# Neighbourhood attention: row sums divided out by GpSimd ahead of the transposes instead of behind the product with V

## The reference, cut to what matters

```python
def hybrid_layer(x, g, w_in, w_out, ...):
    h = rms_norm(x, g)
    z = jnp.einsum('bsd,de->bse', h, w_in)
    ...
    o_da = diff_attention(qd, kd, vd, lam, lam_init, subln_g)
    o_na = neighbourhood_attention(qn, kn, vn, rpb)
    o = jnp.concatenate([o_da, o_na], axis=-1) * jax.nn.silu(gate)
    return x + jnp.einsum('bse,ed->bsd', o, w_out)

    # neighbourhood_attention, for each row of the grid:
    s = q @ kb * scale + bias, masked to the window
    p = jax.nn.softmax(s, axis=-1)
    o = jnp.einsum('bhnqrk,brnkhd->bnqhd', p.astype(v.dtype), vb)
```

## Time and profile before

| what | value |
|---|---|
| median of the runs shown | 1445.77 us (1444.89 to 1445.82) |
| profiled execution, its own time | 1445.27 us |
| span of the profile | 1443.5 us |
| TensorE matmul busy | 1423.7 us, 99% of the span |
| VectorE / ScalarE / GpSimd busy | 882.7 / 687.5 / 494.1 us |
| granted TensorE clock, mean | 0.996 |
| chain that ended last | TensorE 92%, VectorE 3%, ScalarE 2% |

### The profile page before, as it was taken

The page is one execution under the profiler, slowest core; times in us unless marked ns, Lnnn a source line. Parts: engine busy times, 40 slices in busy tenths (PEclk is TensorE's granted clock), DMA queues, the critical chain, the costliest instruction groups (busy, mean ns, idle before and its releaser), DMA issues.

```text
span 1443.5 us, 23727 instructions
## 1 busy us (share of the span) xinstructions
PE 1423.7 (99%) x8180; PEld 1161.4 (80%) x8180; DVE 882.7 (61%) x1827; ACT 687.5 (48%) x1309; POOL 494.1 (34%) x384
## 2 busy tenths in 40 slices
PE   9999999999999999999999999999999999999996
PEld 7788888887888888787887888888878888887875
DVE  6767677667556565653337677666776565656433
ACT  6545554555444444552515554545454444447231
POOL 3223223233333333443642231323233333237152
PEclk9999999999999999999999999999999999999998
DMA  4700101121111111311110110100202121213113
GB/s 182 153 30 27 46 22 36 36 62 38 55 45 49 49 46 47 132 30 58 58 44 30 38 37 15 44 29 22 77 23 63 38 62 36 63 38 124 44 59 117
DMA packets 40698, 79.57 MB, mean 55 GB/s; under 512 B 18992, under 2 KB 19248, under 8 KB 40624
## 3 DMA queue, kind: packets, MB, share of 16 engines
q1 hardware_dynamic: 40480, 78.60, 17.5%
q10 hardware_dynamic: 144, 0.01, 0.0%
HBM read 66.57 MB, written 15.96 MB: 57 GB/s over the span
## 4 chain that ended last, share of the span: by engine, by line
PE 92%; DVE 3%; ACT 2%; DMA 1%; issue 1%; POOL 1%; SPq 0%; POOLq 0%; DVEq 0%; ACTq 0%
PE proj L1041 18%; PE proj L1043 18%; PE proj L1042 18%; PE scores L1077 11%; PE turn L1134 7%; PE mix L1186 3%; PE mix L1187 3%; PE mix L1150 2%; PE mix L1152 2%; PE mix L1151 2%; PE scores L1134 2%; PE mix L1160 1%; DVE pt_lo L1551 1%; DMA xt<-x_t 1%; ACT pt_hi L851 1%
## 5 line engine op out<-in xcount | busy, mean ns | idle before, releaser
L1041 PE MATMUL proj<-h_hi,w_hi 128*128 128x512 f32 x1184 | 491.5, 415 | 2.1 <-DVE h_lo L1426 1.0
L1043 PE MATMUL proj<-h_hi,w_lo 128*128 128x512 f32 x1184 | 465.4, 393 | 0.0
L1042 PE MATMUL proj<-h_lo,w_hi 128*128 128x512 f32 x1184 | 461.8, 390 | 0.0
L626 POOL TENSOR_TENSOR w_lo<-w_raw,w_hi 128x1024 fp32r<-128x1024 f32 x62 | 152.8, 2465 | 502.1 <-ACT w_hi L809 502.1
L1551 DVE TENSOR_TENSOR pt_lo<-turn,pt_hi 128x512 fp32r<-128x512 f32 x208 | 139.1, 669 | 232.2 <-ACT pt_hi L851 231.5
L1043 PEld LDWEIGHTS proj<-h_hi,w_lo 128*128 128x128 f32 x1184 | 222.1, 188 | 50.7
L1041 PEld LDWEIGHTS proj<-h_hi,w_hi 128*128 128x128 f32 x1184 | 223.0, 188 | 47.5 <-issue 9.4
L1042 PEld LDWEIGHTS proj<-h_lo,w_hi 128*128 128x128 f32 x1184 | 223.8, 189 | 34.8
L851 ACT ACTIVATE pt_hi<-turn 128x512 fp32r<-128x512 f32 x208 | 120.2, 578 | 231.0 <-PE turn L1134 229.3
L1543 DVE CUSTOM_DVE_ANT_0 prob<-scores,inner 128x1024 f32<-128x1024 f32 (+1 forms) x192 | 203.5, 1060 | 3.1 <-PE scores L1077 2.7
L876 ACT ACTIVATE prob<-prob,nm,escale_now 128x1024 f32<-128x1024 f32 x128 | 158.4, 1237 | 60.3 <-DVE nm L1547 59.8
(11 more groups left out here) (185 smaller groups left out, 2265.0 us busy)
## 6 DMA issues: line engine op xcount, KB each, us to landing
w_raw<-chunks SPq DMA_DIRECT2D x80, 512.0 KB, 3.5
mixed_dram<-gate SPq DMA_DIRECT2D x28, 256.0 KB, 2.2
edge<-bias_dram SPq DMA_DIRECT2D x32, 224.0 KB, 4.9
h_lo<-mixed_dram SPq DMA_DIRECT2D x14, 512.0 KB, 6.7
xt<-x_t SPq DMA_DIRECT2D x8, 512.0 KB, 8.4
out_t<-xt SPq DMA_DIRECT2D x16, 256.0 KB, 2.1
bias_dram<-bias_rows SPq DMA_DIRECT2D x16, 240.0 KB, 6.1
dist_dram<-inner SPq DMA_DIRECT2D x1, 480.0 KB, 6.5
```

What stands on the lines that cost most here:

```text
L626: pool.tensor_tensor(w_lo[:, b], w_raw[:], f32(w_hi[:, b]), ALU.subtract).then_inc(w_lo_done, 1)
L1041: pe.matmul(dst, a_hi, b_hi, start=start, stop=False)
L1042: pe.matmul(dst, a_hi, b_lo, start=False, stop=False)
L1043: return pe.matmul(dst, a_lo, b_hi, start=False, stop=stop)
```

## The change

GpSimd multiplies the probabilities of each NA tile, both heads, by the reciprocals of their row sums in place (`weigh_rows`), and `turn_p` waits for that product instead of for the exponential. The spread copies, the transposes of the reciprocals and VectorE's product with the gate are dropped. `weigh_rows` stands at the head of GpSimd's step.

```diff
@@ -105,8 +105,6 @@
         for t in range(1, NT + 1):
             for c in range(3 if na and INNER[t - 1] else 2):
                 use(("T", t - 1, c), True)
-            if na and t % 2 == 0:
-                use(("R", t // 2 - 1), False)
         return order, split
 
     def half(t):
@@ -422,7 +420,7 @@
         factor_in = sem("factor_in")
         tails_zero = sem("tails_zero")
         pair_done = sem("pair_done")
-        wide_done = sem("wide_done")
+        prob_scaled = sem("prob_scaled")
 
         f32 = lambda t: t.bitcast(F32)
         HR = NT + NT + 1
@@ -664,18 +662,14 @@
                 pool.wait_ge(gate_plus, 2 * g.group() + t + 1)
                 pool.tensor_tensor(gate[:, cols], gate[:, cols], gate_tanh[:], ALU.mult).then_inc(gate_silu, 1)
 
-            def widen(g, t, before=None):
+            def weigh_rows(g, t):
 
 
                 pool.wait_ge(rrec_done, g.step(t) + 1)
-                if t == 0 and not before.na:
-                    pool.wait_ge(factor_mm, before.kind_pairs(PAIRS - 1) + 1)
-                elif t % 2 == 0:
-                    last = g.use("R", t // 2 - 1) if t else before.use("R", PAIRS - 1)
-                    pool.wait_ge(turned, last + 1)
                 begin(pool, "pool")
-                pool.tensor_copy(rrec_wide[:, t % 2].rearrange("p (m e) -> p m e", e=HD),
-                                 rrec[:, t % 4, :].unsqueeze(2).to_broadcast([P, 2, HD])).then_inc(wide_done, 1)
+                for m in range(2):
+                    part = prob_of(True, t, m, 0, WIDTH[t])
+                    pool.tensor_scalar(part, part, rrec[:, t % 4, m:m + 1], None, ALU.mult).then_inc(prob_scaled, 1)
 
             def normalise(g, p):
 
@@ -688,6 +682,8 @@
 
             def attend(g, behind):
                 for t, front, ft in steps(g, behind):
+                    if front and front.na:
+                        weigh_rows(front, ft)
                     if front and front.projects(ft) and ft % 2 == 0:
                         w_lo_part(front.chunk(ft) + 1, 1 - front.buffer(ft))
                     if g.project and t <= 2:
@@ -696,8 +692,6 @@
                         row_lo(g.l, i)
                     if not behind and t in LAST_CHUNKS:
                         out_lo_part(g.l, LAST_CHUNKS[t])
-                    if front and front.na and t < NT:
-                        widen(front, ft)
                     if t == 1 and not g.project:
                         silu(g, 0)
                     if t == 3 and not g.project:
@@ -710,8 +704,6 @@
                         mask_edge(g.l, behind.i)
                     if t == NT and not g.na:
                         normalise(g, PAIRS - 1)
-                    if front and front.na and t == NT:
-                        widen(front, ft, g)
 
             def norm_stats(n):
                 pool.wait_ge(stat_done, n + 1)
@@ -1121,7 +1113,7 @@
             def turn_p(g, t, c):
                 dst = turn_wait(g, "T", t, c)
                 if g.na:
-                    reached(pe, exp_done, 2 * g.step(t) + min(c, 1) + 1)
+                    pe.wait_ge(prob_scaled, 2 * g.tiles(t) + min(c, 1) + 1)
                 else:
                     pe.wait_ge(comb_done, g.kind_step(t) + 1)
                 if c == 2:
@@ -1187,16 +1179,6 @@
                         last = pe.matmul(out, weights, pt_lo[:, m, at], start=False, stop=n == len(parts) - 1)
                 return last
 
-            def turn_r(g, t):
-
-
-
-                dst = turn_wait(g, "R", t // 2)
-                pe.wait_ge(wide_done, g.tiles(t) + 1)
-                for a in range(2):
-                    last = pe.transpose(dst[:, a * P:(a + 1) * P], rrec_wide[:, a], ident[:])
-                last.then_inc(turned, 1)
-
             def out_piece(l, t, ks):
 
                 n, end = out_number(l, t), NT - 1 if t < EARLY else NT
@@ -1257,8 +1239,6 @@
                     turn_p(g, t - 1, 2)
                 fill(2)
                 if t % 2 == 0:
-                    if g.na:
-                        turn_r(g, t - 1)
                     weigh(g, t - 1)
                 if last_step:
                     turn_v(behind, 0)
@@ -1390,7 +1370,7 @@
                         three(proj[:, q % 2], w_hi[:, b, t // 2], w_lo[:, b, t // 2], h_hi[:, NT - 1, half(t)],
                               h_lo[:, NT - 1, half(t)]).then_inc(piece_done, 1)
                 last_group = Group(l, True, NA_G - 1, project=False)
-                reached(pe, turn_freed, last_group.use("R", PAIRS - 1) + 1)
+                reached(pe, turn_freed, last_group.use("T", NT - 1, 2) + 1)
                 pe.wait_ge(pair_done, last_group.pairs(PAIRS - 1) + 1)
                 if l + 1 == DEPTH:
                     odd = HALVES_LAST[-3:]
@@ -1583,13 +1563,6 @@
                     dve.scalar_tensor_tensor(prob[:, b, :], prob[:, 2, :], cmix[:, b:b + 1], prob[:, b, :],
                                              ALU.mult, ALU.add).then_inc(comb_done, 1)
 
-            def scaled(g, t):
-
-                src, cols = turn_bank(True, ("R", t // 2))[:, 0:2 * P], pair_cols(True, t)
-                dve.wait_ge(turned, g.use("R", t // 2) + 1)
-                dve.wait_ge(gate_silu, 2 * g.group() + TILE[True][t] // 4 + 1)
-                dve.tensor_tensor(gate[:, cols], src, gate[:, cols], ALU.mult).then_inc(turn_freed, 1)
-
             def output_pair(g, t):
 
                 n, cols = (g.l * NA_G + g.i) * PAIRS + t // 2, pair_cols(True, t)
@@ -1597,7 +1570,7 @@
                 dve.tensor_tensor(u_pair[0:HD], mix[0:HD, 0:2 * P], u_pair[0:HD], ALU.add)
                 dve.tensor_tensor(u_pair[HD:P], mix[HD:P, 2 * P:4 * P], u_pair[HD:P], ALU.add).then_inc(u_done, 1)
                 dve.wait_ge(u_done, n + 1)
-                reached(dve, turn_freed, g.use("R", t // 2) + 1)
+                dve.wait_ge(gate_silu, 2 * g.group() + TILE[True][t] // 4 + 1)
                 dve.tensor_tensor(gate[:, cols], u_pair, gate[:, cols], ALU.mult).then_inc(pair_done, 1)
 
             def gated(g, p):
@@ -1659,7 +1632,6 @@
                     piece_part(front, ft)
                 add_pieces(2)
                 if g.na and t % 2 == 0:
-                    scaled(g, t - 1)
                     output_pair(g, t - 1)
                 add_pieces(3)
                 if g.na and t == 1:
```

## The result

The changed kernel takes 1471.66 us (median of four runs, 1469.27 to 1474.47) against 1445.80 us: 25.9 us slower, ratio 1.018, interval 1.0168 to 1.0193. The forecast was 1461.0 us, at most 1470. The direction was right and the size was not.

The account below looks back on a forecast made before the run. TensorE was taken as the bound in ordinary groups, with GpSimd nearly without slack in last groups. Last groups +21.2 us, less 6.0 us taken off TensorE, gave +15.2 us: 1461.0 us, range 1451 to 1470.

Parts of the forecast that it names:

- What bounds the kernel, and where the change binds: TensorE bounds ordinary groups; in each layer's last group GpSimd's rows reach TensorE with 0.4 to 2.4 us to spare.
- What comes off: Transposes of the reciprocals leave TensorE: 26 pairs of 0.23 us not hidden by waits, -6.0 us.
- Ordinary groups hide the products and all that is queued behind them: In ordinary groups, products have 2.3 us to spare and GpSimd work starting up to 3 us later costs nothing.
- The product: One in-place product on GpSimd takes 1.50 us for 512 columns and 1.65 us for 576.
- The nearest row: Profile row for adding a constant over 512 columns on GpSimd, 1497 ns, taken as the product's time.
- the bound from the two copies: Lower estimate of GpSimd's product from copies of 128 and 256 columns: 0.6 us for 512 columns.
- The walk: Tile-by-tile timeline of each last group, products ahead of rows: TensorE shifts 10.6 us a layer, +21.2 us in all.
- The clock: In the last groups TensorE stays busy over two thirds of the time, so no clock fall entered the sum.
- The rival: Clock falls behind last-group waits, 1.9 us each, one or two a layer: 1465 to 1469 us; 0.20 with slower product.
- Most of it isn't the 12 us of products but their place: The last groups' shift comes mostly from rows waiting on GpSimd behind the reciprocals, not from the products' length.

Follow-up runs that it names:

- Run 1: The changed kernel without products in the last group of each layer, whose probabilities stay undivided: 1441.26 us against 1445.49 for the kernel before.
- run 7: The changed kernel with all products on VectorE instead of GpSimd, in ordinary groups too: 1447.91 us, ratio 1.0015.
- run 2: The changed kernel with idle transposes on TensorE ahead of rows 0, 2 and 4 in the last groups, to keep the clock up: 1464.83 us.
- run 4: The changed kernel with every product cut to 64 columns and 34 idle transposes ahead of row 2 in each last group: 1452.27 us.
- run 3: The changed kernel with every product cut to 64 columns, order and waits unchanged: 1456.58 us, ratio 1.0079.

## Why the prediction was wrong, step by step

- **What bounds the kernel, and where the change binds:** right. TensorE is at full clock and without slack in ordinary groups; in both last groups GpSimd has next to no slack. Run 1 places the whole loss there.
- **What comes off, 6.0 us:** right in its working, 3.03 us of 2.99 between the two last groups and 5.52 of 5.52 up to the second, the latter with luck. By the end 4.2 us (medians) or 4.9 us (spans) are left. The prediction had nothing that could take a gain back behind the last group, such as the wait of 0.5 us in run 1.
- **Ordinary groups hide the products and all that is queued behind them:** right. No wait for them there, and run 7 makes no difference by taking the products off GpSimd.
- **The product, 1.50 and 1.65 us:** measured 1.575 and 1.728 us, both some 5% above. The nearest row was the right one, and the bound from the two copies, 0.6 us for 512 columns, was of no use: 64 columns alone take 0.44 us.
- **The walk, 10.6 us a layer:** the mechanism and the waits were right, the term was small. At full clock it is 11.99 us (run 2), and 0.6 us ahead of it, where the products of tile 0 push a split beside VectorE's product with the gate; the walk began at tile 1. The transposes of tile 1 wait 0.8 instead of 0.3 us, and the longer products recur in every step.
- **The clock:** this is the step that failed. The sum had it at nothing, because "In the last group it would stay busy more than two thirds of the time, which speaks against a fall". That sets a mean against single waits of 2 to 4 us. TensorE did stay busy 76% and 77% there, and the clock fell all the same, behind five of the six waits of over 2 us. The falls cost 6.8 us over the two layers (run 2). The rival was there, with 1.9 us for a fall, which is right (1.8), and one or two falls a layer, where the traced execution has two and three; but it had only 0.20, together with a slower product. It was priced on the walk as forecast, 1465 to 1469 us. Its +4 to +8 on the walk as it is (1464.8, run 2) gives 1469 to 1473, and 1471.66 was measured.
- **"Most of it isn't the 12 us of products but their place":** wrong, and at odds with the prediction's own walk, which at no cost of the products had only 2.8 of its 10.6 us. Of 15.2 us a layer over the run without products (1471.66 - 1441.26, halved), 6.3 are length, 5.5 are place with two short products (6.4 by the traces of run 4), 3.4 are clock. Moving the products behind the rows turned one wait into another. GpSimd has more to do in that stretch than fits.

The sum over the kernel before: -4.2 (what comes off, by the end) + 2 x 11.8 (runs 2 less 1) + 6.8 (changed less run 2) = +26.2, against 25.9 us measured (the references of the sets differ by 0.3 us). These are steps between medians, so they have to add up; each step is what a run shows, and the total proves nothing more. By the prediction's terms: 15.2 + 2.4 for the walk + 1.8 for the gain + 6.8 for the clock = 26.2 too.

The Trainium skill's page TensorE: Matmul & The Clock Gate (HAM oscillation) has gaps between matmul bursts bring such a fall. The windows agree: 0.73 us busy of 4.00, and 0.50 granted in the next window. The rate in the Trainium skill's page GPSIMD Engine Reference (section 4.1) for one-input work, roughly line rate, isn't borne out by 1.575 us for 512 columns on GpSimd, where VectorE takes 0.475 us at the least.

## What to carry to other kernels

Before moving work to an engine that is idle two thirds of the time over the whole span, read the one stretch where it isn't: here the last group of each layer, some 36 us twice, holds all of the loss, and leaving those groups alone turns a loss of 1.8% into a gain of 0.4%. When a walk gives waits of several microseconds on TensorE, price the clock's fall behind them as part of the forecast, wait by wait, and not by the mean busy share. Against the run without products in the last groups, reordering the full queue gave back 6 of 30 us here, and moving its new work to another engine 24.

## What was not expected of the hardware

- Idle transposes made a kernel faster: 156 more of them on TensorE, 6.8 us less, with the granted clock at 1.00 where it had been 0.50.
- The length of a single wait didn't settle whether the clock fell: behind 2.26 us it stayed in one layer and fell in the other, with the same code.
- Runs of the changed kernel lie in two pairs, 1469.3 us with a mean clock of 0.990 to 0.992 and 1474.2 us with 0.985, and with the filler within 0.4 us: how much of the time the clock is down differs from run to run. Only one of the four was traced.
- A product of 128x512 by a column of scalars on VectorE takes 0.475 us at the least, and 1.7 to 1.8 us when it starts beside a GpSimd subtraction, with its end 0.3 us behind the subtraction's. The product of output and gate goes the same way in the changed kernel: 0.43 us alone (run 3), 1.27 us beside a split, with its end 0.28 us behind. GpSimd's own time for the product by a column of scalars grows by 1.13 us from 64 to 512 columns, so as an estimate some 0.28 us of it don't depend on the columns.
